# Who copies the turned keys of the latent heads: four PSUM copies of each layer go from ScalarE to VectorE

## The chip, the core and the metric

One core of one Trainium2 chip. The metric is the device time of the whole program in microseconds, lower is better. All arithmetic is in 32-bit floating point.

## What is computed

A first block (a gated delta rule mixer and a mixture of experts) is followed by two layers of a second block. Each of these layers has a mixer with three groups of heads (differential attention, latent attention, a gating unit), a memory cross attention and a convolutional feed-forward part. The change touches the latent attention of both layers. Cut to what matters, the reference is:

```python
def mla_group(cq, ckv, kr, g_cq, g_ckv, w_uq, w_ukv, cos, sin):
    q = (rms_norm(cq, g_cq) @ w_uq).reshape(b, s, MLA_HEADS, MLA_NOPE + MLA_ROPE)
    q = jnp.concatenate([q[..., :MLA_NOPE], apply_rope(q[..., MLA_NOPE:], cos, sin)], axis=-1)
    kv = (rms_norm(ckv, g_ckv) @ w_ukv).reshape(b, s, MLA_HEADS, MLA_NOPE + MLA_V)
    ...
    k = jnp.concatenate([k_nope, jnp.broadcast_to(k_rope, (b, s, MLA_HEADS, MLA_ROPE))], axis=-1)
    o = blocked_attention(q, k, v, (MLA_NOPE + MLA_ROPE) ** -0.5)

def diff_group(...):
    ...
    o = rms_norm(o, g_sub) * (1.0 - lam_init)
```

There are 256 positions, 8 latent heads with queries and keys 96 wide (64 + 32), and 4 differential heads, whose outputs are normalized over 64 columns each.

## The kernel before

Every engine has a program of its own, written out by hand in the order in which it runs (`@block.tensor`, `@block.vector` and so on); the engines meet at counted semaphores. Nothing reorders an engine's instructions. Weights stream through a ring of SBUF slots that SyncE fills ahead of their use.

In each layer l (0 and 1), 16 units of attention u stand in one row: u = 0 to 3 are the differential heads, 4 to 11 the latent heads, 12 to 15 the memory cross attention. One unit goes round like this: TensorE makes the scores (`scores(u)`), VectorE takes the row maxima (`maxima(u)`, L2767 and a small product, L2199), ScalarE makes the exponentials with their row sums (`exps(u)`, L2063), VectorE divides (`normalize(u)`, L2774 and L2199), TensorE turns the probabilities (`turn_p(u)`, L627), ScalarE copies them out of PSUM (`turned(u)`, L2070), TensorE multiplies by the values (`values(u)`), and ScalarE copies the result out (`outs(u)`, L2076 or L2078).

The latent heads need their queries and keys with the 96 channels in partitions. For that TensorE turns them (`turn(k)`, transposes recorded at L627): k = 2 to 5 are the queries (tensor `QT`), 6 to 9 the keys (tensor `KT`), two heads each, into four PSUM buffers (`bank(4 + k % 4)`), 96 partitions by 512 elements. Before, ScalarE copies all eight to SBUF (`turned_in(k)`, L2055), raising the semaphore `tq_ev` by one with each; a whole `tq_ps` says that TensorE is done with one. TensorE's row at this place is: `turn(2)` to `turn(5)`, `values(3)`, `turn(6)` to `turn(9)`, then

```python
pe.wait_ge(tq_ev, tq0 + 10)
scores(4)
scores(5)
```

so the first latent scores wait for the last copy of the keys. After them come `scores(6)`, one job of the memory's keys and values (16 matmuls of 256 columns from the ring) and `turn_p(4)`.

At the same place VectorE waits for `outs(3)` (semaphore `at_oev`), squares the outputs of the differential heads (L2196), sums the squares (L2801, semaphore `ln_ok`), and goes on to `maxima(4)`. ScalarE, behind the copies of the keys, takes the square root of those sums (`root`, L1667), for which it loads another table of functions (ACT_TABLE_LOAD), then loads the table of the exponentials again, and makes `exps(4)`. The root is used much later (VectorE takes it up in unit 5's place).

The tensor names in rows are those of buffers: `ps` is PSUM, `arena` the large SBUF buffer, `small` the small one, `ring` the weights, `cst` constants. L629 and L627 are the lines of one helper (`mm`) that issues every matmul (L629) and every transpose (L627); an `x4` beside a unit's scores or transposes counts records, two to an instruction.

Of the kernel before, what the change touches and what calls it, by code (L numbers as in the profile page):

```python
# [20 lines left out]
T = 256  # L21
# [12 lines left out]
MLA_H, MLA_D, MLA_R = 8, 96, 32  # L34
# [79 lines left out]
def trunk_kernel(nc, stream, par_d, row_d, cst_d, dft_d, xc_d, mem_d, pos_d, sguw_d, out_d):  # L114
    ctx = ExitStack()
    with ctx:
# [3 lines left out]
        def sem(name):  # L120
            return ctx.enter_context(nc.semaphore(name))
# [48 lines left out]
        def bank(b, *dims):  # L170
            n = 1
            for d in dims:
                n *= d
            k = -(-n // 512)
            v = ps[:, b:b + k, :].rearrange("p a b -> p (a b)")[:, 0:n]
            if len(dims) == 2:
                v = v.rearrange("p (a b) -> p a b", a=dims[0])
            elif len(dims) == 3:
                v = v.rearrange("p (a b c) -> p a b c", a=dims[0], b=dims[1])
            return v  # L180
# [46 lines left out]
        def A(at, *dims):  # L227
            return view(arena, at, *dims)
# [92 lines left out]
        QT, KT = A(0, MLA_H, T), A(2048, MLA_H, T)  # L321
# [65 lines left out]
        qk_ok, tq_ps, tq_ev = sem("qk_ok"), sem("tq_ps"), sem("tq_ev")  # L387
# [1241 lines left out]
        def _(act):  # L1629
# [394 lines left out]
            for l in range(LAYERS):  # L2024
# [22 lines left out]
                def turned_in(k):  # L2047

                    act.wait_ge(tq_ps, 10 * l + k + 1)
                    src = bank(4 + k % 4, 2, T)  # L2050
                    if k < 2:
                        A_(dqT if k == 0 else dkT, src, ACT.Copy).then_inc(tq_ev, 1)  # L2052
                    else:
                        dst = (QT if k < 6 else KT)[0:MLA_D, 2 * ((k - 2) % 4):2 * ((k - 2) % 4) + 2, :]
                        A_(dst, src[0:MLA_D], ACT.Copy).then_inc(tq_ev, 1)  # L2055

                def exps(u):
# [14 lines left out]
                def outs(u):  # L2072
                    g = g0 + u
                    act.wait_ge(o2_ps, outs_at(l, u) + 1)
                    if u < 4:
                        A_(ot[:, :, u * 64:u * 64 + 64], bank(2, TT, 64), ACT.Copy).then_inc(o2_ev, 1)  # L2076
                    elif u < 12:
                        A_(cat[:, (u - 4) // 2, :], bank(2, T), ACT.Copy).then_inc(o2_ev, 1)  # L2078
                    else:
                        A_(cat2[:, 2 * (u - 12):2 * (u - 12) + 2, :], bank(2, TT, T), ACT.Copy).then_inc(o2_ev, 1)  # L2080
# [7 lines left out]
                def evac_k(t):  # L2088

                    for n in range(2):  # L2090
# [4 lines left out]
                        late_out(vt[:, t, n * 256:n * 256 + 256].rearrange("p (h d) -> p h d", h=4), src[:, :, 64:128])  # L2095

                turned_in(0)
                turned_in(1)
                exps(0)
                exps(1)  # L2100
# [13 lines left out]
                for k in range(2, 6):  # L2114
                    turned_in(k)
                outs(3)
                for k in range(6, 10):
                    turned_in(k)
                act.wait_ge(ln_ok, 3 * l + 3)
                root(st8, st8, 64).then_inc(sm_ok, 1)  # L2120
                exps(4)
# [67 lines left out]
        def _(dve):  # L2189
            V = nc.vector  # L2190
# [4 lines left out]
            def tt(out, a, b, op=MUL):  # L2195
                return V.tensor_tensor(out, a, b, op)  # L2196

            def ts(out, a, s1, op0, s2=None, op1=None):
                return V.tensor_scalar(out, a, s1, s2, op0, op1) if op1 is not None else V.tensor_scalar(out, a, s1, None, op0)  # L2199
# [242 lines left out]
            for t in range(TT):  # L2442
                dve.wait_ge(kk_ps, 4 + t + 1)
                for d in range(2):
                    k = 2 * (t ^ d) + d
# [191 lines left out]
            for l in range(LAYERS):  # L2637
# [124 lines left out]
                def maxima(u):  # L2762
                    g, q = g0 + u, u % 2
                    dve.wait_ge(sc_ps, g + 1)
                    n = 4 if u < 4 else 2
                    scale = (32 if u < 4 else MLA_D if u < 12 else 256) ** -0.5
                    link(V.tensor_reduce(mx[:, q, 0:n], bank(6 - 2 * q if u < 4 else 4 + u % 4, n, T), axis=AX.X, op=MAX))  # L2767
                    signal(ts(nmx[:, q, 0:n], mx[:, q, 0:n], -scale, MUL), max_ok, False)
# [30 lines left out]
                dve.wait_ge(o2_ev, 12 * l + 4)  # L2799
                link(tt(tmp2, otv, otv))  # L2800
                signal(V.tensor_reduce(st, tmp2, axis=AX.X, op=ADD), ln_ok)  # L2801
                maxima(4)
                maxima(5)
                for u in range(4, 12):
# [202 lines left out]
```

## Time and profile before

| | us |
|---|---|
| median of 3 runs | 1781.43 (1781.35 to 1782.09) |
| the profiled execution, whole | 1783.58 |
| its span, first to last instruction | 1781.70 |
| TensorE busy in the span | 1730.0 (97%) |
| VectorE busy | 812.7 (46%) |
| ScalarE busy | 414.3 (23%) |
| mean granted TensorE clock, as a share of full | 0.995 |

The profiled execution lies 1.9 us over its own span and 2.15 us over the median of the runs. Times in rows are microseconds from the start of the span. In a timeline a row merges instructions of one kind that follow each other; in brackets stands how long the engine sat idle before it and who released it. In the chain of waits each piece is work on the path that ended last; "issue" is time in which nothing that the profile shows was waited for.

### The profile page before, as it was taken

Reading aid. Unit: us, or ns where it says so; the run is one execution under the profiler, and the core shown is the slowest. Engines: PE = TensorE matmul, PEld = TensorE weight load, DVE = VectorE, ACT = ScalarE, POOL = GpSimd, SP = SyncE. Lnnn points to the kernel's source line nnn. Section 1 sums busy time; section 2 is a strip of 40 time slices with the busy share of each in tenths; the row PEclk is TensorE's granted clock in tenths of the full one; section 3 lists DMA queues with packets and bytes.
Section 4 is the critical chain, followed back from the end, with each engine's and each line's share of the span. In section 5 each row is a group of like instructions: output and inputs, shape, how many; then the busy total and the mean of one; then the engine's idle time right before and its main releaser. Section 6 shows DMA issues by size and latency. Waiting matters only on the chain.

```text
span 1781.7 us, 28828 instructions
## 1 busy us (share of the span) xinstructions
PE 1730.0 (97%) x11934; PEld 1400.0 (79%) x11934; DVE 812.7 (46%) x1807; ACT 414.3 (23%) x903; POOL 66.0 (4%) x60
## 2 busy tenths in 40 slices
PE   7999999999999999999999999999999899999997
PEld 4767787666666566679789889999897698899996
DVE  4898444111111111145534445666556344576665
ACT  3743311000000000021632221111314522311112
POOL 1022001000000000010002000000000000000000
PEclk9999999999999999999999999999999999999999
DMA  9111784999999999954224244444433133244420
GB/s 396 75 71 53 301 320 180 396 422 422 422 422 422 422 422 422 421 216 161 100 95 142 95 142 166 160 161 158 156 130 142 61 129 119 95 166 164 160 79 24
DMA packets 53663, 383.52 MB, mean 215 GB/s; under 512 B 6080, under 2 KB 6336, under 8 KB 7360
## 3 DMA queue, kind: packets, MB, share of 16 engines
q1 hardware_dynamic: 52272, 376.91, 54.1%
q10 hardware_dynamic: 1296, 5.24, 0.8%
q8 instruction: 71, 1.16, 0.3%
q14 instruction: 24, 0.20, 0.0%
HBM read 381.08 MB, written 1.05 MB: 214 GB/s over the span
## 4 chain that ended last, share of the span: by engine, by line
PE 92%; DVE 5%; ACT 2%; DMA 1%; issue 0%; POOLq 0%; ACTq 0%; DVEq 0%
PE ps L629 89%; PE ps L627 2%; DVE arena L2196 2%; PE ps L686 1%; DVE arena L2202 1%; DMA xT<-in_xc 1%; DVE small L2767 0%; DVE arena L2612 0%; DVE arena L2199 0%; ACT arena L2055 0%; ACT arena L1742 0%; DVE xT L2196 0%; DVE small L2196 0%; ACT arena L2172 0%; ACT arena L2052 0%
## 5 line engine op out<-in xcount | busy, mean ns | idle before, releaser
L629 PE MATMUL ps<-arena,ring 128*128 128x256 f32 (+2 forms) x3248 | 602.5, 343 | 9.6 <-DVE arena L2196 2.1
L629 PEld LDWEIGHTS ps<-arena,ring 128*128 128x128 f32 x3248 | 507.4, 191 | 83.4 <-issue 38.5
L629 PE MATMUL ps<-ring,arena 128*64 128x256 f32 (+5 forms) x3120 | 459.5, 414 | 0.0
L629 PE MATMUL ps<-arena 128*128 128x128 f32 (+6 forms) x3178 | 416.5, 292 | 4.9 <-ACT arena L2055 1.7
L629 PEld LDWEIGHTS ps<-ring,arena 128*64 128x64 f32 (+1 forms) x3120 | 274.3, 148 | 168.0 <-issue 84.4
L629 PEld LDWEIGHTS ps<-arena 128*128 128x128 f32 (+3 forms) x3178 | 382.2, 191 | 29.4 <-issue 14.0
L2196 DVE TENSOR_TENSOR arena<-arena,ps 128x256 f32<-128x256 f32 (+2 forms) x256 | 98.6, 404 | 208.9 <-ACT arena L1950 202.8
L2202 DVE SCALAR_TENSOR_TENSOR arena<-arena,par 128x255 f32<-128x255 f32 (+1 forms) x282 | 125.7, 488 | 6.5 <-ACT arena L2172 2.3
L629 PE MATMUL ps<-ring 128*128 128x256 f32 (+2 forms) x896 | 113.0, 289 | 0.5 <-issue 0.5
L2667 DVE COPY arena<-ps 128x128 f32<-128x128 f32 x60 | 17.5, 291 | 208.9 <-PE ps L629 208.9
L629 PEld LDWEIGHTS ps<-ring 128*128 128x128 f32 (+2 forms) x896 | 96.1, 153 | 13.2 <-issue 2.0
L2196 DVE TENSOR_TENSOR arena<-arena 128x512 f32<-128x512 f32 (+2 forms) x142 | 79.9, 576 | 48.4 <-ACT arena L2078 14.4
L2172 ACT ACTIVATE arena<-arena,par 128x256 f32<-128x256 f32 x80 | 43.7, 593 | 225.7 <-DVE arena L2196 225.7
L2598 DVE COPY arena<-ps 128x512 f32<-128x512 f32 x16 | 11.1, 692 | 160.9 <-PE ps L629 160.9
L2196 DVE TENSOR_TENSOR arena<-ring 128x512 f32<-128x512 f32 x120 | 82.7, 689 | 2.1
L627 PE MATMUL ps<-cst,arena 128*128 128x128 f32 (+1 forms) x400 | 59.3, 277 | 13.3 <-DVE arena L2196 5.6
L1950 ACT ACTIVATE arena<-ps 128x512 f32<-128x512 f32 x16 | 9.6, 597 | 258.8 <-PE ps L629 258.8
L627 PEld LDWEIGHTS ps<-cst,arena 128*128 128x128 f32 (+1 forms) x400 | 45.9, 142 | 22.9 <-DVE arena L2196 9.3
L2612 DVE RECIPROCAL arena<-arena 128x256 f32<-128x256 f32 x13 | 22.8, 1753 | 86.2 <-ACT arena L1667 86.2
L629 PE MATMUL ps<-arena,cst 128*128 128x256 f32 (+1 forms) x214 | 52.5, 387 | 2.6 <-ACT arena L1980 0.8
L2767 DVE TENSOR_REDUCE small<-ps 128x2 f32<-128x512 f32 (+1 forms) x32 | 26.3, 822 | 62.6 <-PE ps L629 62.6
L2196 DVE TENSOR_TENSOR arena<-ps,small 128x512 f32<-128x512 f32 x46 | 31.5, 691 | 50.3 <-PE ps L629 48.5
(197 smaller groups left out, 1010.9 us busy)
## 6 DMA issues: line engine op xcount, KB each, us to landing
ring<-in_stream SPq DMA_DIRECT2D x358, 1024.0 KB, 10.1
arena<-in_xc ACTq DMA_DIRECT2D x1, 1024.0 KB, 5.9
xT<-in_xc ACTq DMA_DIRECT2D x1, 1024.0 KB, 10.4
arena<-in_mem ACTq DMA_DIRECT2D x1, 1024.0 KB, 4.8
out_y<-xT ACTq DMA_DIRECT2D x2, 512.0 KB, 2.6
ring<-in_dft ACTq DMA_DIRECT2D x1, 512.0 KB, 8.0
arena<-in_sguw ACTq DMA_DIRECT2D x2, 256.0 KB, 2.7
row<-in_row SPq DMA_DIRECT2D x1, 474.0 KB, 24.9
```

What stands on the lines that cost most here:

```text
L627: i = nc.tensor.transpose(out, lhsT, rhs)
L629: i = nc.tensor.matmul(out, lhsT, rhs, start=start, stop=stop, skip_group_check=skip)
L686: mi = nc.tensor.matmul(mod_at(i)[q:q + 32, 0:T], silu_c[:, c, :], wB(s, c, 0, T), start=c < 4, stop=c >= 4, tile_position=(0, q))
L1950: A_(sg, bank(2, 512), ACT.Silu).then_inc(sg_ok, 1)
L2172: a = A_(ca[:, q, k, :], cb[:, q, k, :] if i else bank(2 + k // 2, 2, T)[:, k % 2, :], ACT.Identity, bias=PR(f"fbias{l}")[:, ch:ch + 1], s ...
L2196: return V.tensor_tensor(out, a, b, op)
L2202: return V.scalar_tensor_tensor(out, a, s1, b, op0, op1)
L2598: V.tensor_copy(ytok[:, 4:8, :], bank(3, 4, P)).then_inc(yhigh_ok, 1)
L2612: link(V.reciprocal(rs[:, 0:T], rs[:, 0:T]))
L2667: link(V.tensor_copy(first_p[:, w], m[:, 0, :]))
L2767: link(V.tensor_reduce(mx[:, q, 0:n], bank(6 - 2 * q if u < 4 else 4 + u % 4, n, T), axis=AX.X, op=MAX))
```

## The change

In both layers VectorE makes the four copies of the turned keys (k = 6 to 9), behind the sums of squares and ahead of `maxima(4)`. ScalarE keeps the four copies of the queries and goes from `outs(3)` straight to the root. The copies raise the same semaphore `tq_ev`, and TensorE's program is the same.

```diff
@@ ScalarE @@
                     else:
-                        dst = (QT if k < 6 else KT)[0:MLA_D, 2 * ((k - 2) % 4):2 * ((k - 2) % 4) + 2, :]
+                        dst = QT[0:MLA_D, 2 * (k - 2):2 * (k - 2) + 2, :]
                         A_(dst, src[0:MLA_D], ACT.Copy).then_inc(tq_ev, 1)
...
                 outs(3)
-                for k in range(6, 10):
-                    turned_in(k)
                 act.wait_ge(ln_ok, 3 * l + 3)
                 root(st8, st8, 64).then_inc(sm_ok, 1)
                 exps(4)
@@ VectorE @@
                 signal(V.tensor_reduce(st, tmp2, axis=AX.X, op=ADD), ln_ok)
+                for k in range(6, 10):
+                    dve.wait_ge(tq_ps, 10 * l + k + 1)
+                    V.tensor_copy(KT[0:MLA_D, 2 * (k - 6):2 * (k - 6) + 2, :], bank(4 + k % 4, 2, T)[0:MLA_D])\
+                        .then_inc(tq_ev, 1)
                 maxima(4)
```

VectorE in layer 0, from the squares of the differential heads' outputs on, before:

```order
L2196 TENSOR_TENSOR arena<-arena 128x512 [waits at_oev]
L2801 TENSOR_REDUCE small<-arena 128x8 [waits v_step]
L2767 TENSOR_REDUCE small<-ps 128x2 [waits at_sc,ln_ok]
L2199 TENSOR_SCALAR small<-small 128x2 [waits v_step]
L2767 TENSOR_REDUCE small<-ps 128x2 [waits at_sc]
```

The same place in the changed kernel (its lines count two fewer here):

```order
L2194 TENSOR_TENSOR arena<-arena 128x512 [waits at_oev]
L2799 TENSOR_REDUCE small<-arena 128x8 [waits v_step]
L2802 COPY arena<-ps 96x512 [waits tq_ps,ln_ok]
L2802 COPY arena<-ps 96x512 [waits tq_ps] x3
L2765 TENSOR_REDUCE small<-ps 128x2 [waits at_sc]
L2197 TENSOR_SCALAR small<-small 128x2 [waits v_step]
```

Four copies stand between the sum of squares and the first maxima of the latent heads.

ScalarE in layer 0, from the copy of unit 3's turned probabilities on, before:

```order
L2070 ACTIVATE arena<-ps 128x512 [waits at_pt]
L2055 ACTIVATE arena<-ps 96x512 [waits tq_ps] x4
L2076 ACTIVATE arena<-ps 128x2x64 [waits at_o]
L2055 ACTIVATE arena<-ps 96x512 [waits tq_ps] x4
L1667 ACT_TABLE_LOAD
L1667 ACTIVATE small<-small 128x8 [waits ln_ok]
L2063 ACT_TABLE_LOAD
L2063 ACTIVATE arena,small<-ps,small 128x256 [waits at_max]
```

The same place in the changed kernel:

```order
L2070 ACTIVATE arena<-ps 128x512 [waits at_pt]
L2055 ACTIVATE arena<-ps 96x512 [waits tq_ps] x4
L2076 ACTIVATE arena<-ps 128x2x64 [waits at_o]
L1667 ACT_TABLE_LOAD
L1667 ACTIVATE small<-small 128x8 [waits ln_ok]
L2063 ACT_TABLE_LOAD
L2063 ACTIVATE arena,small<-ps,small 128x256 [waits at_max]
```

The second group of four copies is gone; the two table loads and the root follow on unit 3's output. Layer 1 has the same two differences, and TensorE, GpSimd and SyncE have none.

## Rows read from the trace of the kernel before

**Rows 1.** The page: busy time and share of the span, matmuls.
```profile
PE 1730.0 (97%) x11934; PEld 1400.0 (79%) x11934; DVE 812.7 (46%) x1807; ACT 414.3 (23%) x903; POOL 66.0 (4%) x60
PE 92%; DVE 5%; ACT 2%; DMA 1%; issue 0%; POOLq 0%; ACTq 0%; DVEq 0%
```

**Rows 2.** Chain of waits, layer 0, then layer 1: start, us, what.
```profile
880.25 0.45 PE ps L627 x4
880.70 0.02 issue
880.72 2.06 ACT arena L2055 x4
882.78 0.04 issue
882.83 6.31 PE ps L629 x28
...
1387.77 2.06 ACT arena L2055 x4
```

**Rows 3.** Timeline of TensorE: start, us, line, tiles [idle before <-releaser].
```profile
880.09 1.91 PE L627 MATMUL ps<-cst,arena 128*96 128x128 f32 x16
882.83 2.86 PE L629 MATMUL ps<-arena 96*128 96x256 f32 x12 [0.83 <-ACT arena L2055]
885.52 3.62 PE L629 MATMUL ps<-ring 128*128 128x256 f32 x16
888.98 0.60 PE L627 MATMUL ps<-cst,arena 128*128 128x128 f32 x4
```

**Rows 4.** Timeline of VectorE, layer 0.
```profile
880.60 0.69 DVE L2196 TENSOR_TENSOR arena<-arena 128x512 f32<-128x512 f32 x1 [6.91 <-ACT arena L2076]
881.33 0.69 DVE L2801 TENSOR_REDUCE small<-arena 128x8 f32<-128x512 f32 x1
884.07 0.69 DVE L2767 TENSOR_REDUCE small<-ps 128x2 f32<-128x512 f32 x1 [2.05 <-PE ps L629]
886.86 0.62 DVE L2199 TENSOR_SCALAR arena<-arena,small 128x256 f32<-128x256 f32 x2
890.48 0.69 DVE L2767 TENSOR_REDUCE small<-ps 128x2 f32<-128x512 f32 x1 [1.49 <-PE ps L629]
891.28 0.20 DVE L2607 RECIPROCAL small<-small 128x8 f32<-128x8 f32 x1
```

**Rows 5.** Timeline of ScalarE, layer 0.
```profile
880.72 2.05 ACT L2055 ACTIVATE arena<-ps 96x512 f32<-96x512 f32 x4 [0.16 <-PE ps L627]
882.79 1.28 ACT L1667 ACT_TABLE_LOAD   x1
884.31 1.28 ACT L2063 ACT_TABLE_LOAD   x1
885.61 0.47 ACT L2063 ACTIVATE arena<-ps,small 128x256 f32<-128x256 f32 x1
```

**Rows 6.** Timeline of VectorE: copies and products out of PSUM, a copy out of SBUF.
```profile
148.92 1.41 DVE L2372 COPY ring<-ps 32x512 f32<-32x512 f32 x2
163.74 1.30 DVE L2383 COPY ring<-ps 64x512 f32<-64x512 f32 x2
193.67 3.68 DVE L2196 TENSOR_TENSOR ring<-ps,small 128x512 f32<-128x512 f32 x6
248.45 0.69 DVE L2473 COPY arena<-small 128x1024 f32<-128x1024 f32 x1
```

**Rows 7.** Timeline of TensorE: the same 56 matmuls in layer 0 and layer 1; a pause.
```profile
810.57 6.41 PE L629 MATMUL ps<-ring,arena 128*128 128x32 f32 x56
1314.36 9.51 PE L629 MATMUL ps<-ring,arena 128*128 128x32 f32 x56
1401.17 0.63 PE L627 MATMUL ps<-cst,arena 128*128 128x128 f32 x4 [2.34 <-DVE arena L2199]
```

**Rows 8.** Busy time by stretch; the eighth number from the left is the granted clock (PEclk).
```profile
16.00:20.00 4.00, 3.54 (x16) 2.14 (x20) 1.39 (x2) 1.56 (x2) 0.00 (x0) 0.60 1.02 426
1320.00:1324.00 4.00, 4.00 (x21) 4.00 (x20) 0.00 (x0) 0.01 (x1) 0.00 (x0) 0.50 0.73 262
1398.90:1401.10 2.20, 0.00 (x0) 0.00 (x0) 2.10 (x6) 0.66 (x4) 0.00 (x0) 1.00 0.00 0
```

## The prediction

> **What bounds the kernel now.** I read the page's first and fourth part first: TensorE is busy 97% of the span, and 92% of the chain that ended last is TensorE's work [rows 1]. So a microsecond counts only if TensorE waits for it, and everything that TensorE waits for counts in full. Then I read the chain of waits at the place of the change. There the chain leaves TensorE: its first two transposes of keys end, then come 2.06 us of ScalarE's copies (L2055), then the scores of the latent heads [rows 2]. Layer 1 has the same piece, of the same 2.06 us. The copies are on the path, then, but most of their time lies beside TensorE's other transposes: the timeline of TensorE shows transposes until 880.09 + 1.91 = 882.00 and the scores at 882.83, an idle time of 0.83 us [rows 3]. That 0.83 us in each of two layers, 1.7 us in all, is the most that faster copies could give back here.
>
> Next, the timelines of the two engines that trade work. VectorE is free from 881.33 + 0.69 = 882.02 until 884.07, when the first scores are there [rows 4]. ScalarE starts the copies at 880.72, as soon as the first transpose allows, ends them at 882.77, then loads a table, takes the root, loads the other table, and starts the exponentials at 885.61 [rows 5].
>
> **The copies leave ScalarE.** Four copies of 96x512 took 2.05 us together [rows 5], from 880.72. ScalarE then loads the root's table at about 880.6 instead of 882.79, takes the root when the sums are there (882.05) and has the exponentials' table by about 882.05 + 0.2 + 1.3 = 883.6, against 885.6 before. What is that worth? `exps(4)` waits for the maxima too. Before, these were ready at 884.96 (the first maxima start at 884.07, take 0.69 [rows 4], and their small product adds 0.2), so the table was 0.65 us late. Behind the exponentials comes VectorE's division, and then TensorE's `turn_p(4)`. TensorE arrives there only at 888.98 and does not wait: its row has no idle time in front [rows 3], and the division was over at 886.86 + 0.62 = 887.48 [rows 4], 1.5 us earlier. So 0.65 us off the exponentials hits work that TensorE never waited for. Value of this part: nothing, with 1.5 us of cover. The cover is the job of 16 ring matmuls, 3.62 us long [rows 3], and it stays. The root itself is taken up by VectorE only after the maxima of unit 7, at 891.28 [rows 4], so 2 us less on ScalarE's side change nothing there.
>
> **The copies arrive on VectorE.** They stand behind the squares and the sum of squares, and these wait for ScalarE's `outs(3)`. The first copy cannot start before 882.02, plus 0.03 between instructions: 882.05. ScalarE had by then made two of the four and started the third. So even with no change in price the keys are late by 882.05 - 880.72 = 1.33 us.
>
> The price on VectorE: a copy of this shape is not in the trace, the nearest rows are copies out of PSUM of 64 and 32 partitions by 512. Two of the first took 1.30 us, two of the second 1.41, and one alone takes 0.69 (such durations are the same for 32, 64 and 128 partitions), so the starts are 0.61 to 0.72 apart; six products out of PSUM of the same length took 3.68, which makes (3.68 - 0.69) / 5 = 0.60 apart [rows 6]. I take 0.61, since the pair with 1.30 and the six products start all at one partition as the four copies here do: 3 x 0.61 + 0.69 = 2.52 us. Upper bound, with 0.72 apart: 2.85. Lower bound: a copy out of SBUF moved 1024 elements in the same 0.69 us [rows 6]; if the copies here went at that rate, 512 elements would take about 0.42, some 0.3 apart, 1.3 us in all. I do not take it, because every 512 elements out of PSUM took 0.69.
>
> The Trainium skill (Perfetto Trace Analysis, section Optimizing Scalar/DVE Operations) gives VectorE an overhead of about 125 ns for an instruction that reads PSUM and ScalarE about 51. By that the copies would start 0.66 us apart and take 2.67 in all, 0.15 more than by the rows, and the sum below would be 0.3 us higher; the six products at 0.60 apart speak against it.
>
> The keys are then in SBUF at 882.05 + 2.52 = 884.57. From ScalarE's last copy to the scores it was 0.04 us [rows 2]; I allow 0.04 to 0.14, on average 0.08, for the release by VectorE. The scores start at 884.65 instead of 882.83: **1.8 us later in each layer**. From the bounds: 0.6 us (SBUF rate) to 2.2 us (0.72 apart, slower release).
>
> **Who is queued behind the copies.** On VectorE `maxima(4)`. It needs the scores, which now come later than the copies end by construction, so it does not wait for the copies themselves. From the scores on everything runs in the old rhythm, 1.8 us later: VectorE's next wait for TensorE was 1.49 us at 890.48 [rows 4], so VectorE has slack there and no delay is added; and as it is TensorE that releases it, none of the delay is made up either. Later pauses of TensorE, such as the 2.34 us in layer 1 [rows 7], follow from VectorE's work behind scores that TensorE had just made, and so they move along. Nothing in the trace lets TensorE catch up: it is the bound. No DMA and no queue is moved.
>
> **The sum.** 2 x 1.8 = 3.6 us. The profiled execution, 1783.58 whole and 1781.70 in its span, would be 1785.3 in span and 1787.2 whole. Against the median of the runs, 1781.43, it gives **1785.1**, 0.20% slower.
>
> **Rival 1, the clock falls in the longer pause.** The pause of TensorE grows from 0.83 to about 2.65 us, in both layers. The granted clock fell to the lower level twice in this trace: at 16 to 20 us, after short products and waits, where it was 0.60 of full over 4 us, which costs at most 0.40 x 4 = 1.6 us, and at 1320 to 1324, where it was 0.50 though TensorE was busy throughout [rows 8]; before that it had run products of only 32 columns. The same 56 matmuls took 6.41 us in layer 0 and 9.51 in layer 1 [rows 7], a price of 3.1 us. For this rival: the new pause is longer than the 2.34 us one, the longest in these layers. Against it: across that one the clock stayed 1.00 [rows 8]. One fall gives 1785.1 + 1.6 = 1786.7, two 1788.3. [...]
>
> **Rival 2, the other side: the fall at 1317 goes away.** The identical work fell in layer 1 and not in layer 0, so it hangs on how the work lies in time, and layer 1's copy of it now starts 1.8 us later, by the delay of layer 0. If it no longer falls, 3.1 us come back: 1785.1 - 3.1 = 1782.0, no measurable change. It turns to faster where one layer's delay is under 3.1 / 2 = 1.55 us; with the copies at the SBUF rate, 0.6 us, it would be 1781.4 + 1.2 - 3.1 = 1779.5. Against it: the clock row is of one execution, and the runs agree within 0.74 us, so nothing shows that all of them have this fall.
>
> **Rival 3, the delay is hidden in part.** If VectorE's copies overlapped its sum of squares, or were cheaper than in rows 6, the delay would be 0.6 to 1.5 us a layer: 1782.6 to 1784.4. Rows 4 and 6 speak against it. That the change does not do what it says can be left out: TensorE waits for the same count, and the order shows four copies moved in each layer.
>
> **How the numbers follow.** My forecast 45% (1784.6 to 1785.9 by itself), rival 1 30%, rival 2 13% (of it 4% faster), rival 3 12% (2% faster, by small gains elsewhere). The range to hold 8 in 10 leaves out rival 2's end and the upper end of rival 1: 1782.8 to 1788.0. A measurement of this kernel can tell about 0.2% from no change, 3.56 us, so the line is 1784.99, and my forecast stands almost on it: two thirds of it count as slower. Slower: 0.30 + 0.30 = 0.60. Faster: 0.05, rounded down from 0.06. Within 0.2%: 0.35.
>
> **What would show it.** In the trace after, four copies on VectorE from 882.05 to 884.57, TensorE idle for 2.6 us before the scores instead of 0.83, released by VectorE, and the same 1.8 us later again in layer 1. ScalarE's exponentials would start some 0.9 us after the maxima's start instead of 1.5. `turn_p(4)` has no idle time in front. The forecast is wrong if the pause is under 2.3 us, if another wait of TensorE shrinks, or if the granted clock differs from 1.00 anywhere in 880 to 900 or 1388 to 1410, or from 0.50 at 1320.

## The result, and the profile after

| | before | after |
|---|---|---|
| median, us | 1783.81 (1780.82 to 1789.05, 20 runs) | 1788.72 (1784.05 to 1792.60, 20 runs) |
| ratio | | 1.0030, 95% interval 1.0023 to 1.0036 |
| profiled execution, whole / span, us | 1783.58 / 1781.70 | 1792.38 / 1790.59 |
| TensorE busy | 1730.0 | 1734.9 |
| mean granted clock | 0.995 | 0.993 |

The change makes the kernel slower by 0.30%, 5.4 us by the ratio (4.1 to 6.4) and 4.9 by the medians. The forecast was 1785.1 with a range of 1782.8 to 1788.0; the direction was right, the time lies above the range. With 20 runs instead of three the kernel before itself has a median of 1783.8, not 1781.4. Two terms were mis-sized, then: the base, by 2.4 us, and the cost of the change, at which the fall of TensorE's clock in the longer pauses had been left out of the sum.

The chain of waits of the changed kernel at the place of [rows 2] (start, us, what):

```profile
882.30 0.29 ACT arena L2076
882.59 0.02 issue
882.61 0.70 DVE arena L2194
883.31 0.02 issue
883.34 0.70 DVE small L2799
884.03 0.02 issue
884.06 2.49 DVE arena L2802 x4
886.55 0.04 issue
886.59 6.49 PE ps L629 x21
```

Where ScalarE's 2.06 us stood, the path now runs through unit 3's output copy (ACT L2076), the squares (L2194), the sum of squares (L2799) and VectorE's four copies (L2802), 4.3 us in all. TensorE's timeline in layer 0, then layer 1, beside [rows 3]:

```profile
882.10 1.91 PE L627 MATMUL ps<-cst,arena 128*96 128x128 f32 x16
886.59 4.54 PE L629 MATMUL ps<-arena 96*128 96x256 f32 x12 [2.58 <-DVE arena L2802]
890.97 3.62 PE L629 MATMUL ps<-ring 128*128 128x256 f32 x16
...
1395.44 5.49 PE L629 MATMUL ps<-arena 96*128 96x256 f32 x12 [2.58 <-DVE arena L2802]
1400.73 4.35 PE L629 MATMUL ps<-ring 128*128 128x256 f32 x16
```

Two things are to be seen. The pause is 2.58 us instead of 0.83, 1.75 more in each layer. And the same twelve records of scores behind it take 4.54 and 5.49 us instead of 2.86: the products themselves have become slower. The busy time by stretch says why (the eighth number from the left is the granted clock):

```profile
884.00:886.60 2.60, 0.02 (x2) 0.01 (x1) 2.50 (x5) 1.49 (x2) 0.00 (x0) 1.00 0.01 3
886.80:890.20 3.40, 3.40 (x9) 2.69 (x9) 0.86 (x2) 0.73 (x3) 0.00 (x0) 0.50 0.00 0
1395.40:1402.20 6.80, 6.75 (x16) 5.34 (x17) 3.56 (x11) 2.04 (x8) 0.00 (x0) 0.50 0.00 0
```

After TensorE had stood idle for 2.6 us its clock fell to the lower level, 1.2 GHz, for 3.4 us in layer 0 and 6.8 in layer 1, just when the scores began. ScalarE got what the change gives it, and it was worth nothing:

```profile
882.60 1.28 ACT L1667 ACT_TABLE_LOAD   x1
884.06 0.21 ACT L1667 ACTIVATE small<-small 128x8 f32<-128x8 f32 x1 [0.18 <-DVE small L2799]
884.28 1.28 ACT L2063 ACT_TABLE_LOAD   x1
889.47 0.47 ACT L2063 ACTIVATE arena<-ps,small 128x256 f32<-128x256 f32 x1 [3.90 <-DVE small L2197]
```

The exponentials' table is ready at 885.56, and then ScalarE idles 3.90 us for the maxima of scores that had not been made.

**How the time is parted below.** Every run in the table below is one execution and lists its span and its mean granted clock. Span times clock is the time at the full clock; the rest of the span is lost to the lower clock (about 3 to 4 us of it at the very end, where TensorE is done). The clock is given to three digits, so a single run is good to 0.9 us and only means are used. For the 28 to 33 runs of the kernel before, the standard error is 0.1 us at the full clock and 0.3 of the lost time; for 10 or 11 runs of another kernel it is 0.1 to 0.3 and up to 1.0. The parting itself is rough, since a fall during an idle stretch counts as lost too: where the pauses tell what the time at the full clock should be, it comes out up to 0.8 us off (e1).

| kernel | runs | mean, us | at the full clock | lost to the clock |
|---|---|---|---|---|
| before, beside e1 to e4 | 33 | 1783.49 | 1773.58 | 8.10 |
| before, beside e5 to e8 | 28 | 1783.15 | 1773.84 | 7.51 |
| before, beside e9 to e12 | 30 | 1782.77 | 1773.59 | 7.36 |
| changed (first measurement) | 20 | 1788.35 | 1777.33 | 9.20 |
| e5, changed, again | 10 | 1788.32 | 1777.59 | 8.94 |

Over all 30 runs of the changed kernel and 91 of the kernel before, the difference is 3.75 us at the full clock (3.50 by the two pauses) and 1.4 us more lost to the clock, with a standard error of 0.5.

### The profile page after: what moved, and what is told of

Its sections match the earlier page's. It is cut to its first block, busy times and chain, and to the rows that moved or that the text cites. A ratio compares the mean times of both kernels' runs of the same rounds, so it can differ in the third digit from the quotient of the medians.

```text
span 1790.6 us, 28828 instructions
## 1 busy us (share of the span) xinstructions
PE 1734.9 (97%) x11934; PEld 1403.5 (78%) x11934; DVE 817.8 (46%) x1815; ACT 410.4 (23%) x895; POOL 66.0 (4%) x60
## 4 chain that ended last, share of the span: by engine, by line
PE 92%; DVE 5%; ACT 1%; DMA 1%; issue 1%; POOLq 0%; ACTq 0%; DVEq 0%
PE ps L629 89%; PE ps L627 2%; DVE arena L2194 2%; PE ps L686 1%; DVE arena L2200 1%; DMA xT<-in_xc 1%; DVE small L2765 0%; DVE arena L2610 0%; DVE arena L2802 0%; DVE arena L2197 0%; ACT arena L1742 0%; DVE xT L2194 0%; DVE small L2194 0%; ACT arena L2170 0%; ACT arena L2052 0%
## 5 line engine op out<-in xcount | busy, mean ns | idle before, releaser
L2194 DVE TENSOR_TENSOR arena<-arena,ps 128x256 f32<-128x256 f32 (+2 forms) x256 | 98.5, 404 | 208.9 <-ACT arena L1950 202.8
L2194 DVE TENSOR_TENSOR arena<-arena 128x512 f32<-128x512 f32 (+2 forms) x142 | 79.8, 575 | 48.5 <-ACT arena L2078 14.4
L2194 DVE TENSOR_TENSOR arena<-ring 128x512 f32<-128x512 f32 x120 | 82.6, 689 | 2.1
L2194 DVE TENSOR_TENSOR arena<-ps,small 128x512 f32<-128x512 f32 x46 | 31.5, 691 | 50.3 <-PE ps L629 48.5
```

## Experiments

Theory: the keys come 1.75 us late in each layer, because the copies stand behind 1.4 us of squares and sums and because VectorE starts one every 0.6 us; TensorE waits for the last of them; and in the longer pause its clock falls in part of the executions. Rivals: VectorE's speed alone, delays further down the chain, or a fall of the clock that has nothing to do with the pause.

**e1 and e9, filled pauses.** In both layers of the changed kernel:

```diff
+                idle_products(3, 9)
                 pe.wait_ge(tq_ev, tq0 + 10)
                 scores(4)
```

> The changed kernel, with nine idle products (128x128, into a free PSUM buffer, 1.9 us) that TensorE runs ahead of its wait for the keys, in both layers; the scores can start no earlier by them. Theory (the late copies cost 1.75 us a layer, and a clock fall in the pause costs the rest): the pause of 2.6 us shrinks to about 0.65, the scores start at the same distance behind the transposes, the granted clock stays 1.00 there, and the kernel is 3.5 us over the kernel before (ratio 1.0020) instead of the 4.9 to 5.4 of the changed kernel, with less scatter. Rival (the excess over 3.5 us is a cost of the copies that falls elsewhere, the clock only happens to fall there in the profiled execution): 4.9 to 5.4 us over, as without the products.

> The changed kernel with nine idle products in both new pauses, once more. In the first run it lost only 4.5 us to the lower clock, 3.6 less than the kernel before beside it, although the three idle products in the pause of the kernel before changed nothing. Theory (the pauses' part of the loss is 1.1 to 1.4 us, the rest of that gap was chance in where the falls lay): at the full clock 3.5 to 4 us over, lost to the clock within 1 us of the kernel before, 3 to 4 us over in all (ratio 1.0017 to 1.0023). Rival (the filled pauses really save more): again about 1.4 us over, with about 3.5 us less lost than the kernel before.

Measured: 1784.20 against 1782.80, ratio 1.0005 (0.9996 to 1.0014), and 1784.21 against 1782.46, ratio 1.0006 (0.9998 to 1.0015). TensorE's timeline in e1, layer 0, and a stretch there:

```profile
880.60 2.17 PE L629 MATMUL ps<-cst 128*128 128x128 f32 x18
883.35 2.86 PE L629 MATMUL ps<-arena 96*128 96x256 f32 x12 [0.57 <-DVE arena L2803]
```
```profile
884.00:888.00 4.00, 4.00 (x21) 3.50 (x20) 3.12 (x9) 1.93 (x8) 0.00 (x0) 1.00 0.00 0
```

The scores wait as long as before (the last transpose ends at 880.76, 2.59 us ahead), but run at the full clock, in 2.86 us. At the full clock they are 4.3 and 3.6 us over the kernel before, where the pauses ask for 3.5. Lost to the clock were 4.54 and 5.02 us, 3.9 to 4.7 less than the changed kernel. So work that does nothing for the result takes back 4 of the 5 us, all of it in the time lost to the clock. That is more than expected: e1 was to bring 1.4 to 1.9 us and e9 1.1 to 1.4, and in e9 the rival came out. The filled kernel loses even less than the kernel before (3.6 and 2.3 us less), though the kernel before has only its short pauses there. The pauses alone can't explain this; the table under e13 to e16 comes back to it.

**e2, the place without the order.** VectorE makes the copies ahead of the squares, with a semaphore of their own:

```diff
+                for k in range(6, 10):
+                    dve.wait_ge(tq_ps, 10 * l + k + 1)
+                    V.tensor_copy(KT[...], bank(...)[0:MLA_D]).then_inc(kt_ev, 1)
                 dve.wait_ge(o2_ev, 12 * l + 4)
                 link(tt(tmp2, otv, otv))
                 signal(V.tensor_reduce(st, tmp2, axis=AX.X, op=ADD), ln_ok)
```

> The changed kernel, but VectorE makes the four copies ahead of the squares and the sum of squares (with a semaphore of their own, the arithmetic is the same). This parts the price of the place from the price of the engine. Theory: of the 1.75 us a layer 1.33 come from the place (behind 1.42 us of squares and sums) and 0.4 from VectorE's 0.6 us a copy against ScalarE's 0.49. The copies start at outs(3) or the first transpose, about 0.1 us after 880.7, and end about 2.5 us later; the pause of TensorE is 1.2 to 1.3 us instead of 0.83, no clock fall there, and the kernel is 0.9 us over the kernel before (ratio 1.0005). Rival (VectorE's slower copies are what costs): 3.5 us over.

Measured: 1783.60 against 1782.80, ratio 1.0007 (0.9998 to 1.0016); 0.83 us over at the full clock, none more lost. VectorE's and TensorE's rows, layer 0:

```profile
881.47 2.48 DVE L2799 COPY arena<-ps 96x512 f32<-96x512 f32 x4 [7.04 <-PE ps L627]
883.87 0.68 DVE L2194 TENSOR_TENSOR arena<-arena 128x512 f32<-128x512 f32 x1
```
```profile
884.01 2.86 PE L629 MATMUL ps<-arena 96*128 96x256 f32 x12 [1.26 <-DVE arena L2799]
```

Pause 1.26 us: 0.43 are the engine's price, and the other 1.32 of the 1.75 the place behind the squares.

**e11, the place without the engine.** ScalarE makes all copies but waits for the sums ahead of the keys:

```diff
+                act.wait_ge(ln_ok, 3 * l + 3)
                 for k in range(6, 10):
                     turned_in(k)
-                act.wait_ge(ln_ok, 3 * l + 3)
                 root(st8, st8, 64).then_inc(sm_ok, 1)
```

> The kernel before with ScalarE making all copies, but waiting for VectorE's sum of squares ahead of the four copies of the keys: the place of the change without its engine. Theory: the copies start at 882.05 instead of 880.72 in the time of the kernel before, 1.33 us later, and take their 2.05 us; the pause of TensorE is 2.16 us instead of 0.83, 2.7 us over at the full clock in two layers, and some falls of the clock in the pauses, 3 to 4 us over in all (ratio 1.0017 to 1.0022). Rival (VectorE is what costs): under 1 us over.

Measured: 1784.60 against 1782.46, ratio 1.0017 (1.0006 to 1.0029); 3.2 us over at the full clock. TensorE, layer 0:

```profile
886.09 4.54 PE L629 MATMUL ps<-arena 96*128 96x256 f32 x12 [2.15 <-ACT arena L2055]
```

A pause of 2.15 us, 1.32 more than before, as forecast, with no key copied by VectorE; and here too the clock fell behind it (4.54 us for the scores), so the fall does not hang on who copies. In layer 1 of the same execution it did not fall behind the same pause, and over the 12 runs no more was lost to the clock than in the kernel before (0.2 us less, standard error 0.9), so the falls that were expected here do not show in the mean. e2 and e11 together are the 1.75 us: 0.43 for the engine and 1.32 for the place.

**e10, layer 0 alone.**

```diff
-                for k in range(6, 10):
+                for k in range(6, 6 if l else 10):
                     dve.wait_ge(tq_ps, 10 * l + k + 1)
```

(and ScalarE keeps its four copies where l is 1)

> The change in layer 0 alone; in layer 1 ScalarE makes the copies of the keys as before. Theory (each layer pays for itself): the pause is 2.58 us in layer 0 and 0.83 in layer 1; half of the excess, 1.75 to 1.9 us at the full clock and 0.5 to 0.8 us by the clock, about 2.4 us over the kernel before (ratio 1.0014). Rival (one layer's delay only moves the other's work against the clock): anything between 0 and 4 us.

Measured: 1786.17 against 1782.46, ratio 1.0015 (1.0006 to 1.0025); 1.5 us over at the full clock, 0.9 more lost. The pauses are 2.58 and 0.83 us. Half the change costs half, within the interval. TensorE in layer 0:

```profile
883.68 2.86 PE L629 MATMUL ps<-arena 96*128 96x256 f32 x12 [2.58 <-DVE arena L2804]
```

Here the clock stayed up behind the pause of 2.58 us: the scores took 2.86 us.

**e3 and e4, a split wait.** TensorE waits copy by copy, and the buffers of the turned heads are shifted by two, so that unit u writes into the one whose copy it has waited for. Once on the changed kernel (e3), once on the kernel before (e4):

```diff
-                pe.wait_ge(tq_ev, tq0 + 10)
+                pe.wait_ge(tq_ev, tq0 + 7)
                 scores(4)
+                pe.wait_ge(tq_ev, tq0 + 8)
                 scores(5)
                 for u in range(4, 12):
                     if u + 2 < 12:
+                        if u < 6:
+                            pe.wait_ge(tq_ev, tq0 + 5 + u)
                         scores(u + 2)
...
-                    b = 4 + k % 4
+                    b = 4 + (k if k < 2 else k + 2) % 4
```

> The changed kernel, with VectorE's copies where the change has them, but TensorE's one wait for all four copies is split: scores(4) waits for the first, scores(5) for the second, scores(6) for the third, scores(7) for the fourth; the PSUM buffers of the turned queries and keys are shifted by two, so that the buffer of unit u is the one emptied by the copy that it waits for. Theory (only TensorE's wait for the last copy makes the place of the copies cost anything): the first copy ends 0.75 us after TensorE's last transpose, the pause is about 0.8 us as before the change, and the kernel equals the kernel before (ratio 0.9995 to 1.0005). Rival (VectorE's later maxima delay the chain too): 1 to 3.5 us over.

> The kernel before, copies on ScalarE, with the same split of TensorE's wait and the same shift of the PSUM buffers. Theory: the first copy is made before the last transpose ends, so the pause of 0.83 us goes in both layers, and nothing else waits: 1.7 us under the kernel before (ratio 0.9991), turn_p(4) comes 0.83 us earlier and still finds its probabilities. Rival (the exponentials are bound by the table load, so TensorE's gain comes back as a wait at turn_p(4)): no difference.

Measured for e3: 1783.48 against 1782.80, ratio 0.9999 (0.9990 to 1.0008); for e4: 1780.24, ratio 0.9982 (0.9973 to 0.9991). TensorE in layer 0 of e3, then of e4:

```profile
881.25 2.86 PE L629 MATMUL ps<-arena 96*128 96x256 f32 x12 [0.79 <-DVE arena L2805]
```
```profile
878.81 1.91 PE L627 MATMUL ps<-cst,arena 128*96 128x128 f32 x16
880.55 2.76 PE L629 MATMUL ps<-arena 96*128 96x256 f32 x12
```

In e3 the copies stand where the change puts them and run just as long, and the kernel is no slower than the kernel before: the change's 5 us came through TensorE's wait for the last copy. In e4 the pause is gone, 1.0 us a layer from the first transpose of keys to the scores, 2.2 us at the full clock and 1.2 less lost. So the split does not make the two engines equal. With the same split on both sides, the copies behind VectorE's squares still cost 1.8 us at the full clock (e3 against e4) and 2.6 us by the means, because TensorE waits 0.79 us in each layer for the first of them, and not at all where ScalarE makes it. The best of the four kernels is the split wait with the copies left on ScalarE.

**e5, the changed kernel again.**

> The changed kernel as it is, once more, beside the kernel before on the same chip, to part its excess into time at the full clock (span times mean granted clock) and time lost to the lower clock (the rest of the span). Theory: at the full clock 3.5 us over (two times 1.75), and 1 to 2 us more lost to the clock than before, 4.5 to 5.5 us in all (ratio 1.0025 to 1.0031). Rival (the clock is lost alike in both kernels, the rest is something else): at the full clock 4.9 us over, nothing more lost.

Measured: 1789.16 against 1783.44, ratio 1.0027 (1.0016 to 1.0037); 3.75 us over at the full clock and 1.4 more lost (standard error 1.0), as in the first measurement. Its profiled execution shows the same pause without a fall in layer 0 and with one in layer 1:

```profile
884.97 2.86 PE L629 MATMUL ps<-arena 96*128 96x256 f32 x12 [2.58 <-DVE arena L2802]
1392.16 4.54 PE L629 MATMUL ps<-arena 96*128 96x256 f32 x12 [2.58 <-DVE arena L2802]
```

**e6 and e7, filled pauses in the kernel before.** e6 has three idle products ahead of the latent scores in both layers, e7 nine ahead of `turn_p(6)` in layer 1:

```diff
-                    if u == 0:
-                        idle_products(3, 7)
+                    if u == 0 or u == 6 and l == 1:
+                        idle_products(3, 9 if u else 7)
```

> The kernel before with three idle products (0.65 us) in its own pause of 0.83 us ahead of the latent scores, in both layers. Theory: this pause is too short for the clock to fall, so nothing changes (ratio 0.9997 to 1.0003). Rival (the kernel before too loses clock there in some executions, which would explain that the changed kernel with filled pauses came out only 1.4 us over): 1 to 2 us under the kernel before, by less lost to the clock.

> The kernel before with nine idle products (1.9 us) in the 2.34 us pause ahead of turn_p(6) in layer 1. The clock fell there in all four profiled executions of the first experiments. Theory: the time lost to the clock drops by 0.8 to 1.7 us, the time at the full clock stays within 0.3 us of before (ratio 0.9991 to 0.9996). Rival (the fall costs nothing since TensorE's work there is bound by VectorE anyway): no change.

Measured for e6: 1783.93 against 1783.44, ratio 1.0000 (0.9991 to 1.0009). For e7: 1782.68, ratio 0.9995 (0.9986 to 1.0004), 0.4 us less lost: the sign that was expected, inside the noise. Filling the 0.83 us pause changes nothing, so it costs no clock that these runs can see.

**e8 and e12, three edits on the kernel before.** The split wait of e4, the nine products of e7, and the 16 products of 32 columns, which stood in a row in [rows 7], put in pairs behind the eight wide products of the same slot (24 records of 32 columns that belong to other products stay in a row):

```diff
+                        b, b2 = late_bank(), late_bank()
+                        for c in range(KC):
+                            mm(bank(b, T), wA(s, c, 0), h[:, c, :], ...)
+                            for i in (2 * c, 2 * c + 1):
+                                t, cc = i // KC, i % KC
+                                mm(bank(b2, TT * 32)[:, t * 32:t * 32 + 32], h[:, cc, t * P:t * P + P], wB(s, cc, P, 32), ...)
```

> The kernel before with three edits: the split wait with shifted buffers (as in the fourth experiment), the nine idle products ahead of turn_p(6) in layer 1, and the 16 products of 32 columns (the turned rope keys) each pair behind one wide product of the same slot instead of in a row. Theory (three separate costs that add up): 1.98 us less at the full clock, 0.8 to 1.7 us less lost ahead of turn_p(6), and 1 to 2 us less lost behind the narrow products, 4 to 5 us under the kernel before (ratio 0.9972 to 0.9978), with less scatter. Rival (the clock falls move elsewhere): 2 us under.

> The kernel of the eighth experiment once more, for a closer interval. Theory: 4.5 to 6 us under the kernel before (ratio 0.9967 to 0.9975), no clock fall ahead of turn_p(6) or behind the narrow products. Rival (the first run was a lucky one): 2 to 3 us under.

Measured: 1777.88 against 1783.44, ratio 0.9969 (0.9957 to 0.9981), and 1777.57 against 1782.46, ratio 0.9970 (0.9959 to 0.9982). At the full clock 2.1 and 2.0 us less, lost 3.1 and 2.6 us less. Of the 5.2 and 4.5 us by the means, the split wait alone had brought 3.4 (e4) and the nine products alone 0.7, inside the noise (e7); the narrow products were not moved alone, so what they bring is not shown. Two stretches of e8, at the narrow products of layer 0 and at the former pause of layer 1:

```profile
812.00:816.00 4.00, 4.00 (x36) 3.95 (x35) 0.00 (x0) 1.75 (x3) 0.00 (x0) 1.00 0.23 51
1394.00:1398.00 4.00, 3.89 (x24) 3.39 (x23) 2.19 (x8) 0.60 (x1) 0.00 (x0) 1.00 0.00 0
```

This kernel beats both, by 0.3% against the one before and 0.6% against the changed one (by the two ratios, 0.9970 / 1.0030). In the profiled execution of e8 no fall of the clock lies between the start's idle products and TensorE's end; in that of e12 the only one is at the start, from 16.6 us on and 10.2 us long.

**e13 to e16, where the clock falls.** The kernel before (e13, e15) and the changed one with filled pauses (e14, e16), unaltered, one execution each.

> One look at the kernel before, for where the granted clock falls. Theory (the narrow products of one layer or of the other meet the fall, since the two layers lie differently against the clock's own rhythm): one fall at 812 to 820 or at 1315 to 1325. Rival: none at both.

> One look at the changed kernel with filled pauses. Theory (layer 1 lies 1.75 us later against layer 0, and both layers now meet the clock alike): a fall behind the narrow products of both layers or of neither. Rival: of one alone, as in the kernel before.

> A second look at the kernel before. Theory: one fall at 812 to 820 or at 1315 to 1325. Rival: none at both.

> A second look at the changed kernel with filled pauses. Theory: a fall behind the narrow products of both layers or of neither. Rival: of one alone.

Where the granted clock fell between the start's first 20 us and the end of TensorE's work, in all profiled executions of these kernels (us from the start of the span):

| kernel | falls |
|---|---|
| before | 1317 |
| before, e13 | 1399 |
| before, e15 | 813, 1318, 1400 |
| before with e6's products | 154, 1318, 1400 |
| changed | 815, 887, 1324, 1395 |
| changed, e5 | 1321, 1392, 1406 |
| changed, filled: e1 | 1401 |
| changed, filled: e9 | none |
| changed, filled: e14 | 1401 |
| changed, filled: e16 | 814 |
| e2, place without the order | 1399 |
| e3, changed, split wait | 1397 |
| e4, before, split wait | 1315, 1397 |
| e7, before, nine products in layer 1 | 282, 1317 |
| e10, layer 0 alone | none |
| e11, late copies on ScalarE | 815, 887 |
| e8 and e12, three edits | none in either, besides e12's at the start |

In both executions of the changed kernel the clock fell at the pause in layer 1, in one of the two in layer 0. Taken together, the seven open pauses of 2.15 or 2.58 us ahead of the latent scores (changed, e5, e10, e11) had a fall behind them four times, the eight filled ones never, and the pauses of 0.79 to 1.26 us there never. That is what ties the fall to the long pause.

It does not account for all that the filled kernel saves. The idea behind e13 and e14, that the distance between the layers decides whether the narrow products meet a fall, does not hold: e15 has falls in the narrow products of both layers, e16 in those of layer 0 alone. What remains is that 3 of 4 executions with the old pauses fell at 1317 to 1318 and none of the 4 filled ones did, though that stretch of the program is the same. The start differs in the same way: a fall at 16 to 17 us stood in two of the three executions of the kernel before and in both of the changed one, and in none of the four filled ones, though nothing that the edit touches has run by then. So at least that part comes from how the executions happened to lie, and why the filled kernel loses less than the kernel before is open.

## Why the prediction was wrong, point by point

- **What bounds the kernel; whose wait it is.** Right. The chain after runs through the copies, and TensorE's wait for them is released by VectorE.
- **The copies on VectorE, 2.52 us from 882.05 on.** Right: 2.48 us (0.60 apart), starting 0.03 us behind the sum. The release took 0.04 us, not the 0.08 that I took. The estimate of 2.67 us from the overhead of 125 ns that the Trainium skill gives VectorE for reading PSUM (Perfetto Trace Analysis, section Optimizing Scalar/DVE Operations) was too high: the copies started 0.60 us apart, not 0.66, as the six products had said.
- **1.8 us later a layer, 3.6 in all.** Right within its rounding: 1.75 and 3.50 in the pauses; e2 and e11 part it into 0.43 for the engine and 1.32 for the place, where the prediction had 0.47 (2.52 less 2.05) and 1.33.
- **ScalarE's lead is worth nothing.** Right; it idled 3.90 us behind its table load. `turn_p(4)` had no idle time in front.
- **Nothing further down gives back or adds.** Right at the full clock: from the scores of layer 0 to the first keys' transpose of layer 1 it took 501.06 us where the clock did not fall, in e1, e2, e3, e9, e10, e13 and e16 alike (501.08 in e14).
- **The base.** This failed, and it is the larger part of the miss. 1781.43 was the median of three runs that lay in the lower half of what the kernel before does; 20 runs gave 1783.81. The three agreed within 0.74 us, and I took that as the width of a measurement. A fourth execution lay before me, the profiled one with 1783.58, 1.5 us over the highest of the three, and I took its distance for something that belongs to profiling. It does not: over the twelve kernels with several runs, the profiled execution was 0.5 us faster than the mean of the others (standard error 0.7). 1783.81 + 3.6 is 1787.4, inside the range; 2.4 of the 3.6 us between 1785.1 and 1788.7 are the base.
- **Rival 1, the clock.** This is the other 1.2 us, and the step that failed is its weighing: the sum put the clock's cost at nothing. I gave the fall 30% as a thing that happens or not, and spoke against it with a row in which the clock stayed 1.00 across a pause of 2.34 us [rows 8]. That row was one execution. Of 14 others that have that pause open, the clock fell right behind it in nine (e1 to e6, e13 to e15) and not in five. It is a cost that some executions pay and some don't, 1.6 to 1.7 us for each 3.4 us at the lower level, so it belonged in the sum with its mean. For the changed kernel that mean is 1.4 us (standard error 0.5); e11, with pauses of 2.15 us, shows none. The prediction's own sign came out: the clock differed from 1.00 behind both new pauses. The Trainium skill (TensorE: Matmul & The Clock Gate, section Why this matters for your kernels) asks for no idle gaps between bursts beyond a length that none of these pauses reaches; the clock fell behind pauses of 2.15, 2.34 and 2.58 us all the same, and the measurement decides.
- **Rival 2, the fall at 1317 goes away.** Not in either profiled execution of the changed kernel (1324 and 1321). But the fall is no fixed part of the kernel before either: e13 does not have it.

## What to carry to other kernels

Before a step moves to an idle engine, look at what stands ahead of it in that engine's order: here the 1.3 us of place cost three times the 0.43 us by which the new engine is slower. Let each consumer wait only for the part that it needs: here that made up for the late copies, and with the copies left on ScalarE it made the kernel faster than it was before. A pause of the bound engine has two prices, its length and what the clock does after it, and the second shows only over many executions. When three runs agree closely, that is still no measure of how far the kernel's executions lie apart.

## What the runs showed of the hardware

- The granted clock falls in different places in executions of the same kernel, with a step of 1.6 to 1.7 us in the time for each 3.4 us at the lower level (501.06, 502.69 and 504.36 us for the same work between the layers, with none, one and two, in e13, e15 and the changed kernel). This makes most of the scatter: over 91 runs of the kernel before, the standard deviation of the span is 1.5 us, and 0.6 at the full clock, rounding included.
- It fell while TensorE was busy without a gap, in rows of products of 32 columns (between 812 and 819 and between 1315 and 1328 us), in 11 of 32 such rows in 16 profiled executions. With each pair behind a wide product it fell in none of four (e8, e12), too few to show that the order did it.
- With nine idle products in each pause of 2.6 us the clock fell in none of the eight filled pauses of four executions, against four of seven open ones, and the kernel was 4 us faster, 0.2%, without moving a useful instruction. Part of these 4 us lies elsewhere than in the pauses and is not explained.
